# Values of three attention branches with tokens stationary, joined in two passes, and earlier last copies of a bank in the groups of seven products

## The chip, the cores and the metric

One core of one Trainium2 chip runs the whole program. The metric is device time in microseconds, from one launch, lower is better. TensorE (PE) does the matrix products, VectorE (DVE) and ScalarE (ACT) do the elementwise work, GpSimd (POOL) clears a few pads, SyncE (SP) issues the loads.

## The reference, cut to what matters

Two layers over 512 tokens with 1024 features, in float32. Each layer is half a SwiGLU step, a mixer of three attention branches, and another half SwiGLU step:

```
h = h + 0.5 * SwiGLU_1(RMSNorm(h))
u = RMSNorm(h);  z = u @ w_in        # a_q a_k a_v | b_q b_k b_v b_f | c_q c_k c_v | gates
A: differential attention (4 heads of 128), B: forgetting attention (8 heads of 64),
C: stick-breaking attention (8 heads of 64), all causal
m = sum_i sigmoid(gate_i) * (o_i @ proj_i);  h = h + m @ w_out
h = h + 0.5 * SwiGLU_2(RMSNorm(h))
```

Each of the queries, keys and values of a branch has 512 columns. The row scale of RMSNorm (`rstd`) is one number a token, and the gain is folded into `u`.

## The kernel before, in words

**Layout and precision.** Activations stand as features x tokens: 128 partitions, 512 token columns, eight such tiles for 1024 features. A float32 product is made of three rounded products (`three`, lines 713 to 717): each factor is kept as a rounded part (`_hi`) and the rest (`_lo`), and hi x hi, hi x lo and lo x hi are added in one PSUM bank. ACT makes the rounded part and DVE the rest, of weights too: `split(k)` is one ACT copy and one DVE subtraction of 128x1024 for one weight slot. There are three slots, each holding one *unit*, the 8 blocks of 128x128 that make 128 output columns of `w_in`. A unit on PE is 24 products of 512 columns.

**A tile of the mixer.** There are four tiles a layer, each with 128 columns of every branch (one head pair of B and of C, one head of A), and two layers, so eight tiles in all. Each tile has nine units: c_q, c_k, c_v, b_q, b_k, b_v, a_q, a_k, a_v (a letter for the branch). Their banks alternate between 0 and 1. When a unit is done, DVE's `take` multiplies the bank by `rstd` into one of two staging tiles. Queries and keys then get `qk_hi` on ACT (four copies of 64x512 for b and a) and `qk_lo` on DVE (two subtractions of 64x512), and `scores` waits on `qk_set` for both of its branch. Values stand as features x tokens after the unit but are needed as tokens x features: `turn_values` transposes the staging tile by four float32 transposes into the bank AUX, and `values_hi` and `values_lo` round it.

**Orders written by hand.** PE, ACT and DVE each have an order written out (`heads` and `rest_of_tile` in each engine's block), and each engine runs its order strictly. On PE the attention steps (`stick_scores` for C, `scores` for A and B, `turn_probs`, ten transposes of the weights; `weighted`, the product with the values) are placed between blocks of the units, so that ACT and DVE make the softmax or the stick-breaking weights while PE works on units. `weighted(branch, 1)` is followed on ACT by `output_rest(1)` and on DVE by `output_whole(1)`, which add the two halves of a result.

**Groups of seven products.** In the SwiGLU parts and for the gates, a 2x2 scheme needs seven products in place of eight (`pair`, line 760; `product` is 12 products of 256 columns). Products 0, 2, 4 and 6 add to one bank, and after 0, 2 and 4 ACT copies the bank away (`snap` 0, 2 and 3, line 1388; snap 1 is for another bank); PE waits for the copy before it adds the next one. ACT also makes the weight pieces of the next group (`piece_hi`), which wait for DVE's sums of weights. `pair_hi` (line 1394) is ACT's order for the SwiGLU, `gates_hi` for the gates.

Of the kernel before, what the change touches and what calls it, by code (L numbers as in the profile page):

```python
# [194 lines left out]
def trunk(nc, x, stream, params, const, const_r, const_b, out):  # L195
    ctx = ExitStack()
    with ctx:
# [12 lines left out]
        O_HI, O_LO = 0, 3 * NT * SEQ  # L210
        QK = 2 * O_LO
# [74 lines left out]
        def val_block(branch, part, j):  # L286
            return val(branch, part)[:, j * P:(j + 1) * P]
# [168 lines left out]
        mean_log, row_rstd = stat[:, 0:2], stat[:, 2:4]  # L456

# [58 lines left out]
        turned = sem("turned")  # L516
# [191 lines left out]
        def _(pe):  # L708
            c = Counts(pe, [acc_lo_set, g_part_set, snap_set, w_set, u_set, acc_set, rstd_set, hid_set, g_set, h_set, wf_set, staged,
                            rows_set, qk_set, v_set, max_set, prob_set, pt_set, o_sq, o_rstd, o_norm,  # L710
# [280 lines left out]
            def turn_values(st):  # L991

                for j in range(NQ):
                    last = pe.transpose(ps[:, AUX, j * P:(j + 1) * P], tile(st)[:, j * P:(j + 1) * P], ident)  # L994
                last.then_inc(turned, 1)
# [7 lines left out]
            def weighted_whole():  # L1003

                pe.wait_ge(v_set, c.next(v_set))

                pe.wait_ge(o_whole_set, c.next(o_whole_set))
                for j in range(NQ):
                    pe.wait_ge(pt_set, c.next(pt_set))
                    n, w_hi_j, w_lo_j = wide_keys(j)  # L1010
                    last = three(ps[:, OB, SEQ - n:SEQ], val_block(0, 0, j), val_block(0, 1, j), w_hi_j, w_lo_j,
                                 start=j == 0, stop=j == NQ - 1)
                last.then_inc(o_mm, 1)

            def weighted(branch, hd, before=True):

                if hd == 0:
                    pe.wait_ge(v_set, c.next(v_set))
# [7 lines left out]
                for j in range(NQ):  # L1026
                    pe.wait_ge(pt_set, c.next(pt_set))
                    n, w_hi_j, w_lo_j = wide_keys(j)
                    v = val_block(branch, hd, j)
# [20 lines left out]
            def unit(k, first_block=0, end=UNIT, first=False, before=True):  # L1050

                if first_block == 0 and (k > 1 or k == 0 and before):

                    pe.wait_ge(staged, c.next(staged, 1 if k else 2))
                last = u_unit(k % 2, k % SLOTS, (first_block, end), first)
# [3 lines left out]
            def rest_of_tile(unit):  # L1059

                unit(0)
                turn_probs(1)
                turn_values(0)
                unit(1, 0, 3)
                weighted(1, 1)
                scores(0, 0)
                unit(1, 3, 7)
                scores(0, 1)
                unit(1, 7)
                c.skip(max_set, NQ)  # L1070

            def heads(before):

                if before:
                    rest_of_tile(unit)
                    unit(2)
                    turn_probs(0)
                    unit(3, 0, 3)
                    weighted_whole()
                    unit(3, 3, 5)  # L1080
                else:
                    unit(0, first=True, before=False)
                    pe.wait_ge(const_set, 1)
                    sum_of_squares()
                    unit(1, 0, 3)
                    forget()
                    unit(1, 3)
                    unit(2)
                    pe.wait_ge(pads_set, c.next(pads_set, 4))
                stick_scores(0)  # L1090
                if before:
                    unit(3, 5, 6)
# [5 lines left out]
                turn_values(0)  # L1098
# [12 lines left out]
                unit(7, 4)  # L1111
                unit(8, 0, 2)
                turn_probs(0)
                turn_values(1)
                unit(8, 2)
                weighted(1, 0)
# [5 lines left out]
            def mixer():  # L1122
                heads(False)
                for _t in range(1, NT):
                    heads(True)

                def gate(k, first_block=0, end=UNIT):
                    if (k, first_block) == (0, 0):
                        pe.wait_ge(staged, c.next(staged, 2))
                    last = u_unit(k, k, (first_block, end))  # L1130
                    if end == UNIT:
                        last.then_inc(unit_done, 1)

                rest_of_tile(gate)
                pe.wait_ge(v_set, c.peek(v_set))
                gate(2, 0, 7)
                turn_probs(0)
                gate(2, 7)
# [4 lines left out]
                weighted_whole()  # L1143
# [5 lines left out]
            def branch_product(k0, b0, of, n, k):  # L1149
# [3 lines left out]
                if b == 0:  # L1153
                    pe.wait_ge(w_set, c.next(w_set))
                at = (branch * NT + k) * SEQ
                last = three(ps[:, of[n], :], slot(w_hi, s, b), slot(w_lo, s, b),
                             area[:, O_HI + at:O_HI + at + SEQ], area[:, O_LO + at:O_LO + at + SEQ],
# [117 lines left out]
        def half_tile(hd):  # L1275

            return ps[:, AUX, :].rearrange("p (j e) -> p j e", j=NQ)[:, :, hd * HEAD:(hd + 1) * HEAD]

        def half_val(branch, hd, part):

            at = HEAD * (hd ^ part)
            return val(branch, hd).rearrange("p (j e) -> p j e", j=NQ)[:, :, at:at + HEAD]

# [1871 lines left out]
```

## Time and profile before

| what | value |
|---|---|
| median of 3 runs | 2438.66 us (2438.55 to 2438.97) |
| the profiled execution's own time | 2438.91 us |
| its span | 2437.1 us |
| PE busy | 2425.9 us, 15514 products |
| DVE busy | 2130.1 us |
| ACT busy | 1493.9 us |
| granted PE clock, mean | 0.999 |
| chain that ended last, share on PE | 94% |

Products are pipelined: the duration of one (390 ns for 512 columns) is longer than the distance between the starts of two. What a product costs is the distance of starts, which the rows of a timeline show. A merged row shows the start of the first and the time to the end of the last.

### The profile page before, as it was taken

How to read it: one execution, taken by the hardware profiler on the slowest of the kernel's cores; microseconds unless marked ns; L12 is line 12 of the kernel's file. 1: busy time of each engine (PE TensorE's matmuls, PEld its weight loads, DVE VectorE, ACT ScalarE, POOL GpSimd, SP SyncE). 2: the span in 40 equal slices, each digit the busy share in tenths (PEclk: the TensorE clock that was granted, in tenths of full speed). 3: DMA queues.
4: the chain of work that ended last, by engine and by line, in shares of the span. 5: the costliest groups of instructions: out<-in, count | busy, mean ns of one | idle time of the engine just before them, and what ended most of it. 6: DMA issues, size and time to landing. Idle time of an engine off the chain costs nothing.

```text
span 2437.1 us, 48108 instructions
## 1 busy us (share of the span) xinstructions
PE 2425.9 (100%) x15514; PEld 2210.7 (91%) x15514; DVE 2130.1 (87%) x3960; ACT 1493.9 (61%) x2917; POOL 4.0 (0%) x14
## 2 busy tenths in 40 slices
PE   9999999999999999999999999999999999999999
PEld 7999888888899889998889998888888998899988
DVE  8999878998898779998699997789998986899985
ACT  7666357888754456664366664578886554566643
POOL 0000000000000000000000000000000000000000
PEclk9999999999999999999999999999999999999999
DMA  4333332212232323233333323322212333233332
GB/s 168 108 103 104 113 97 69 77 55 78 62 113 79 112 87 105 104 106 117 102 103 106 103 95 106 103 79 61 72 60 70 105 106 102 87 107 104 117 113 78
DMA packets 64676, 233.72 MB, mean 96 GB/s; under 512 B 7168, under 2 KB 7552, under 8 KB 64512
## 3 DMA queue, kind: packets, MB, share of 16 engines
q1 hardware_dynamic: 64368, 231.58, 29.3%
q8 instruction: 85, 1.39, 0.2%
q14 instruction: 79, 0.65, 0.1%
q10 hardware_dynamic: 144, 0.10, 0.0%
HBM read 229.55 MB, written 2.10 MB: 95 GB/s over the span
## 4 chain that ended last, share of the span: by engine, by line
PE 94%; DVE 3%; ACT 1%; issue 1%; DMA 0%; DVEq 0%; SPq 0%; ACTq 0%
PE ps L715 29%; PE ps L717 29%; PE ps L716 29%; PE ps L988 2%; PE ps L1031 1%; PE ps L978 1%; PE ps L979 1%; PE ps L1030 1%; DVE w_lo L1990 1%; ACT w_hi L1293 0%; PE ps L994 0%; PE ps L1042 0%; PE ps L1043 0%; DMA h<-x 0%; DVE u_lo L1990 0%
## 5 line engine op out<-in xcount | busy, mean ns | idle before, releaser
L1293 ACT ACTIVATE w_hi<-w_raw 128x512 fp32r<-128x512 f32 (+1 forms) x874 | 624.1, 721 | 470.6 <-PE ps L717 231.3
L1990 DVE TENSOR_TENSOR w_lo<-w_raw,w_hi 128x512 fp32r<-128x512 f32 (+1 forms) x874 | 699.2, 805 | 108.2 <-ACT w_hi L1293 91.8
L715 PE MATMUL ps<-u_hi,w_hi 128*128 128x256 f32 (+1 forms) x2432 | 786.1, 323 | 0.6 <-DVE w_lo L1990 0.6
L717 PE MATMUL ps<-u_hi,w_lo 128*128 128x256 f32 (+1 forms) x2432 | 781.0, 321 | 0.0
L716 PE MATMUL ps<-u_lo,w_hi 128*128 128x256 f32 (+1 forms) x2432 | 780.2, 321 | 0.0
L716 PE MATMUL ps<-area,w_hi 128*128 128x256 f32 (+1 forms) x1778 | 583.4, 328 | 0.0
L715 PEld LDWEIGHTS ps<-u_hi,w_hi 128*128 128x128 f32 x2432 | 463.3, 190 | 37.4 <-issue 2.3
L717 PEld LDWEIGHTS ps<-u_hi,w_lo 128*128 128x128 f32 x2432 | 463.2, 190 | 35.1
L716 PEld LDWEIGHTS ps<-u_lo,w_hi 128*128 128x128 f32 x2432 | 463.5, 191 | 32.8
L715 PE MATMUL ps<-area,w_hi 128*128 128x512 f32 (+1 forms) x1414 | 482.0, 341 | 2.4 <-ACT scratch_whole L1392 1.8
L717 PE MATMUL ps<-area,w_lo 128*128 128x512 f32 (+1 forms) x1414 | 480.1, 340 | 0.0
L716 PEld LDWEIGHTS ps<-area,w_hi 128*128 128x128 f32 x1778 | 338.1, 190 | 29.0
L715 PEld LDWEIGHTS ps<-area,w_hi 128*128 128x128 f32 x1414 | 268.2, 190 | 34.2 <-ACT scratch_whole L1392 1.8
L717 PEld LDWEIGHTS ps<-area,w_lo 128*128 128x128 f32 x1414 | 268.1, 190 | 29.6
L715 PE MATMUL ps<-v_area,w_hi 128*128 128x256 f32 x880 | 249.3, 283 | 0.0
L717 PE MATMUL ps<-v_area,w_lo 128*128 128x256 f32 x880 | 249.0, 283 | 0.0
L1392 ACT ACTIVATE scratch_whole<-ps 128x256 f32<-128x256 f32 x376 | 141.6, 377 | 159.9 <-PE ps L717 158.3
L715 PEld LDWEIGHTS ps<-v_area,w_hi 128*128 128x128 f32 x880 | 168.9, 192 | 0.2
L717 PEld LDWEIGHTS ps<-v_area,w_lo 128*128 128x128 f32 x880 | 168.9, 192 | 0.0
L1293 ACT ACTIVATE area<-scratch_whole 64x512 fp32r<-64x512 f32 (+1 forms) x202 | 123.7, 627 | 25.4 <-DVE scratch_whole L2896 11.8
L716 PE MATMUL ps<-v_area,w_hi 128*128 128x256 f32 x440 | 124.5, 283 | 0.0
L1990 DVE TENSOR_TENSOR area<-scratch_whole,area 64x512 fp32r<-64x512 f32 (+1 forms) x120 | 82.3, 685 | 16.1 <-ACT area L1293 14.0
(220 smaller groups left out, 2909.4 us busy)
## 6 DMA issues: line engine op xcount, KB each, us to landing
w_raw<-weights SPq DMA_DIRECT2D x432, 512.0 KB, 3.7
h<-x SPq DMA_DIRECT2D x4, 512.0 KB, 6.4
out<-scratch_whole SPq DMA_DIRECT2D x8, 256.0 KB, 2.0
scratch_whole<-const_b SPq DMA_DIRECT2D x1, 512.0 KB, 9.6
scratch_whole<-const_r SPq DMA_DIRECT2D x1, 192.0 KB, 8.9
cst<-const SPq DMA_DIRECT2D x1, 137.0 KB, 8.0
par<-params ACTq DMA_DIRECT2D x1, 98.0 KB, 4.5
```

Source lines behind the costliest of these rows:

```text
L715: pe.matmul(dst, hi, x_hi, start=start, stop=False, **kw)
L716: pe.matmul(dst, hi, x_lo, start=False, stop=False, **kw)
L717: return pe.matmul(dst, lo, x_hi, start=False, stop=stop, **kw)
L978: pe.matmul(dst, q_twice(branch, hd)[:, m], k_both(branch, hd)[:, 0:n], start=True, stop=False)
L979: pe.matmul(dst, q_rest(branch, hd)[:, m], k_bias(branch, hd)[:, 0:n], start=False, stop=True).then_inc(score_set, 1)
L988: last = pe.transpose(ps[:, SB0 + j, (i - j) * P:(i - j + 1) * P], prob[buf][:, at:at + P], ident)
L1030: pe.matmul(ps[:, OB, SEQ - n:SEQ], v, w_hi_j, start=j == 0, stop=False)
L1031: last = pe.matmul(ps[:, OB, SEQ - n:SEQ], v, w_lo_j, start=False, stop=j == NQ - 1)
L1293: return act.activation(dst, src, ACT.Copy)
L1392: act.activation(to, half_bank((of or banks(s))[2 if n == 1 else 0]), ACT.Copy).then_inc(snap_set, 1)
L1990: return dve.tensor_tensor(dst, src, hi_part.bitcast(F32), ALU.subtract)
```

## The change: what it does

It has two parts.

**One: values.** The three value units of a tile are joined. The stationary operand is now a block of 128 tokens of `u` (hi or lo), the moving one is the weights of all three branches, 384 columns, so the result comes out as tokens x features and `turn_values` is gone. With 8 feature blocks and 4 token blocks these are 32 steps of three products (`value_steps`), in two passes: token blocks 0 and 1, then 2 and 3. At feature block 2 the 384 weight columns wrap around the end of the slots, and the step is made of three products of 256 columns and three of 128. `values_hi` and `values_lo` now read four banks, in halves of 128x128 and 128x256, and scale by `token_rstd`, one number a partition, which PE gets once a layer by four transposes of `rstd` (`turn_rstd`). The stream of weights has a new order: c_q, c_k, the joined values in three units, b_q, b_k, a_q, a_k. Staging is by `take(k, bank, scale)`: queries in staging tile 0, keys in 1. All three hand-written orders of a tile change with it.

**Two: last copies.** In `pair_hi` for the first group of a SwiGLU, and in `gates_hi` for its first two groups, `snap` 3 comes ahead of the copy of weight piece 3 (and, in the very first group of the program, ahead of piece 2).

PE's order, the middle of a tile:

```
                     diff_norm()
-                unit(3, 6 if before else 0)
-                unit(4, 0, 6)
+                value_steps(20 if before else 11, 30, before)
+                turn_probs(0)
+                value_steps(30, 32, before)
                 ...
-                turn_values(0)
+                own = (AUX, 0, 1, AUX) if before else (0, AUX, 1, AUX)
+                unit(own[0], 2, 0, 5)
+                weighted(t, 2, 0, before)
+                stick_scores(1)
+                unit(own[0], 2, 5)
+                unit(own[1], 0)
                 turn_probs(0)
-                unit(4, 6)
-                unit(5, 0, 4)
-                weighted(2, 0, before)
-                stick_scores(1)
-                unit(5, 4)
-                unit(6, 0, 7)
+                unit(own[2], 1, 0, 5)
+                weighted(t, 2, 1)
+                scores(1, 0)
+                unit(own[2], 1, 5)
+                bank_read(1 if before else 2)
+                unit(own[3], 2, 0, 3)
                 turn_probs(0)
-                unit(6, 7)
-                unit(7, 0, 4)
-                weighted(2, 1)
-                scores(1, 0)
-                ...
```

ACT's order, after the stick-breaking of the second head:

```
                 act.preload_act_table_set(LN_EXP)
-                qk_hi(1, 2, 4)
+                qk_hi(1, 0, 0)
                 split(2)
                 turned_hi(0)
                 ...
                 turned_hi(3)
+                qk_hi(1, 2, 1)
                 split(0)
                 output_rest(1)
```

DVE's order at the same place:

```
                 output_whole(0)
-                qk_lo(1, 0, 3)
                 stick_runs(0)
                 ...
                 stick_weights(3)
-                take(5, 1.0)
+                banks = (AUX, 0, 1, AUX) if before else (0, AUX, 1, AUX)
+                take(0, banks[0], SCALE)
                 rows(t * 2, 1, 0)
-                qk_lo(1, 2, 4)
                 split(2)
+                qk_lo(1, 0, 0)
                 turned_lo(0)
                 ...
                 turned_lo(3)
-                take(6, SCALE)
+                take(1, banks[1], 1.0)
                 split(0)
                 output_whole(1)
+                qk_lo(1, 2, 1)
                 block_max(0, 0)
```

The new function on PE, and part two in `pair_hi`:

```
+            def value_steps(begin, end, before):
+                for n in range(begin, end):
+                    late, m = divmod(n, 2 * UNIT)
+                    k, j = m // 2, 2 * late + m % 2
+                    ...
+                    for first, after in ((0, 2), (2, 3)) if k == 2 else ((0, 3),):
+                        ...
+                        pe.matmul(dst, x_hi, w_hi[:, of], start=k == 0, stop=False, skip_group_check=True)
+                        pe.matmul(dst, x_lo, w_hi[:, of], start=False, stop=False, skip_group_check=True)
+                        last = pe.matmul(dst, x_hi, w_lo[:, of], start=False, stop=k == UNIT - 1, skip_group_check=True)

                 piece_hi(2, raws(s))
+                if first and not early:
+                    product_done()
+                    product_done()
+                    snap(s, 3)
                 hidden_hi(at - 2 * SEQ)
-                product_done()
+                if not first:
+                    product_done()
                 piece_hi(3, raws(s))
-                product_done()
-                snap(s, 3)
+                if not first:
+                    product_done()
+                    snap(s, 3)
```

## Rows read from the trace of the kernel before

**Rows 1.** The page: span, and busy time by engine.

```profile
span 2437.1 us, 48108 instructions
PE 2425.9 (100%) x15514; PEld 2210.7 (91%) x15514; DVE 2130.1 (87%) x3960; ACT 1493.9 (61%) x2917; POOL 4.0 (0%) x14
```

**Rows 2.** Waits of PE: total us, times, longest us.

```profile
PE ps L715 <- ACT scratch_whole L1392: 1.8, 2, 1.6
```

**Rows 3.** Timeline of PE, values turned: start us, us, engine, line, operation.

```profile
383.68 0.39 PE L717 MATMUL ps<-u_hi,w_lo 128*128 128x512 f32 x1
...
384.36 0.39 PE L717 MATMUL ps<-u_hi,w_lo 128*128 128x512 f32 x1
384.60 0.60 PE L994 MATMUL ps<-cst,scratch_whole 128*128 128x128 f32 x4
385.03 1.25 PE L988 MATMUL ps<-cst,scratch_whole 128*128 128x128 f32 x10
386.04 0.47 PE L715 MATMUL ps<-u_hi,w_hi 128*128 128x512 f32 x1
```

**Rows 4.** Timeline of PE, a later tile, the middle of it.

```profile
533.67 0.33 PE L1030 MATMUL ps<-area,v_area 128*128 128x384 f32 x1
533.84 0.34 PE L1031 MATMUL ps<-area,v_area 128*128 128x384 f32 x1
...
534.50 0.28 PE L1042 MATMUL ps<-area 128*128 128x256 f32 x1
...
543.29 1.25 PE L988 MATMUL ps<-cst,scratch_whole 128*128 128x128 f32 x10
...
549.10 0.28 PE L978 MATMUL ps<-area 128*128 128x256 f32 x1
```

**Rows 5.** Timeline of ACT in the same stretch.

```profile
540.40 2.31 ACT L1293 ACTIVATE area<-scratch_whole 64x512 fp32r<-64x512 f32 x4
542.74 1.06 ACT L1293 ACTIVATE w_hi<-w_raw 128x1024 fp32r<-128x1024 f32 x1
...
549.30 0.59 ACT L1656 ACTIVATE w_raw<-ps 64x512 f32<-64x512 f32 x1 [2.35 <-PE ps L1031]
```

**Rows 6.** Timeline of DVE in the same stretch.

```profile
538.37 1.00 DVE L2580 TENSOR_TENSOR_SCAN scratch_whole<-scratch_whole,masks 128x127 f32<-128x127 f32 x2
...
542.87 0.68 DVE L2510 SCALAR_TENSOR_TENSOR scratch_whole<-ps,rstd 128x512 f32<-128x512 f32 x1
...
544.11 1.39 DVE L1990 TENSOR_TENSOR area<-scratch_whole,area 64x512 fp32r<-64x512 f32 x2
545.52 1.23 DVE L1990 TENSOR_TENSOR w_lo<-w_raw,w_hi 128x1024 fp32r<-128x1024 f32 x1
546.66 1.68 DVE L1990 TENSOR_TENSOR area<-ps,area 128x512 fp32r<-128x512 f32 x4
548.26 0.68 DVE L2510 SCALAR_TENSOR_TENSOR scratch_whole<-ps,rstd 128x512 f32<-128x512 f32 x1
...
550.10 0.69 DVE L2625 TENSOR_TENSOR w_raw<-ps,w_raw 64x512 f32<-64x512 f32 x1
```

**Rows 7.** Timeline of PE at the start of the program.

```profile
3.18 5.58 PE L1225 MATMUL ps<-area 128*128 128x512 f32 x14 [3.18 <-issue]
8.60 0.40 PE L715 MATMUL ps<-u_hi,w_hi 128*128 128x512 f32 x1
```

**Rows 8.** Timeline of PE in the first group of seven products.

```profile
51.62 0.28 PE L717 MATMUL ps<-u_hi,w_lo 128*128 128x256 f32 x1
53.50 0.39 PE L715 MATMUL ps<-area,w_hi 128*128 128x256 f32 x1 [1.60 <-ACT scratch_whole L1392]
```

**Rows 9.** The same, first group of a later SwiGLU.

```profile
918.81 0.28 PE L716 MATMUL ps<-u_lo,w_hi 128*128 128x256 f32 x1
918.93 0.28 PE L717 MATMUL ps<-u_hi,w_lo 128*128 128x256 f32 x1
919.36 0.38 PE L715 MATMUL ps<-area,w_hi 128*128 128x256 f32 x1
```

More of the change, by code:

```diff
@@ L1048, in diff_norm, with unit @@
                 pe.matmul(ps[:, bank, :], ones_r[:], o_sq_lo, start=False, stop=True).then_inc(o_ms, 1)
[L1050 to L1055, printed above, removed]
+            def unit(bank, k, first_block=0, end=UNIT, first=False):
+                last = u_unit(bank, k, (first_block, end), first)
@@ L1117, in heads @@
+                unit(own[2], 1, 5)
+                bank_read(1 if before else 2)
+                unit(own[3], 2, 0, 3)
+                turn_probs(0)
+                unit(own[3], 2, 3)
+                weighted(t, 1, 0)
                 scores(1, 1)
@@ L1122, in mixer @@
             def mixer():
[L1123 to L1136, printed above, removed]
+                heads(0, False)
+                for t in range(1, NT):
+                    heads(t, True)
+                rest_of_tile(NT - 1, unit)
+                bank_read()
+                unit(2, 2, 0, 7)
                 turn_probs(0)
-                gate(2, 7)
+                unit(2, 2, 7)
                 pe.wait_ge(o_set, c.peek(o_set, 3 * NT - 2))
@@ L1602, in key_bias, with qk_hi @@
                         hi(k_bias(branch, hd)[half(1 - hd), :], key_sums[half(1 - hd), :])
-            def qk_hi(branch, which, k, takes=1):
-                act.wait_ge(staged, c.next(staged, takes))
+            def qk_hi(branch, which, k):
+                act.wait_ge(staged, c.next(staged))
                 for hd in range(2):
-                    src = tile(k % 2)[half(hd), :]
+                    src = tile(k)[half(hd), :]
                     if which == 0:
@@ L2463, in forget @@
                 dve.wait_ge(rstd_set, c.next(rstd_set))
-                stage_qk(2, 0, 0)
+                take(0, 0, SCALE, first=True)
+                split(0)
+                qk_lo(2, 0, 0)
                 y, soft, neg, run = tile(3), tile(2), tile(6), tile(4)
@@ L2475, in forget @@
                 dve.wait_ge(vec_done, c.next(vec_done))
-                take(1, 1.0)
+                take(1, 1, 1.0, first=True)
+                split(1)
                 dve.wait_ge(forget_out, layer * 2 + 1)
@@ L2499, in sums_of_forget, with take @@
                 dve.wait_ge(vec_done, c.next(vec_done))
-            def stage(k, scale):
-                take(k, scale)
-                split(k % SLOTS)
-            def take(k, scale):
-                if k >= 2:
+            def take(k, bank, scale, first=False):
+                if not first:
                     dve.wait_ge(qk_set, c.peek(qk_set, 0))
                 dve.wait_ge(unit_done, c.next(unit_done))
-                dve.scalar_tensor_tensor(tile(k % 2), ps[:, k % 2, :], scale, rstd[:], ALU.mult, ALU.mult
-                                         ).then_inc(staged, 1)
-            def stage_qk(branch, which, k):
-                stage(k, SCALE if which == 0 else 1.0)
-                qk_lo(branch, which, k)
+                dve.scalar_tensor_tensor(tile(k), ps[:, bank, :], scale, rstd[:], ALU.mult, ALU.mult).then_inc(staged, 1)
             def qk_lo(branch, which, k):
@@ L2613, in output_lo @@
             def output_lo(branch, t):
-                at = (t + branch * NT) * SEQ
+                rounded, rest = (area[:, o_at(branch, t, part):o_at(branch, t + 1, part)] for part in range(2))
                 src = o_whole[:]
@@ L2703, in heads @@
                 stick_weights(3)
-                take(5, 1.0)
+                banks = (AUX, 0, 1, AUX) if before else (0, AUX, 1, AUX)
+                take(0, banks[0], SCALE)
                 rows(t * 2, 1, 0)
-                qk_lo(1, 2, 4)
                 split(2)
+                qk_lo(1, 0, 0)
                 turned_lo(0)
@@ L3099, in weight_stream, with unit @@
         for t in range(NT):
-            for name in "cba":
-                for which in range(3):
-                    parts.append(columns(w_in, branch[name] + which * 512 + t * P))
+            def unit(name, which):
+                return columns(w_in, branch[name] + which * 512 + t * P)
+            values = np.concatenate([unit(name, 2) for name in "abc"], 0).transpose(1, 2, 0, 3)
+            parts += [unit("c", 0), unit("c", 1), values.reshape(P, 3, UNIT, P).transpose(1, 0, 2, 3)]
+            parts += [unit(name, which) for name in "ba" for which in range(2)]
         proj = np.concatenate([a[f"proj_{'abc'[b]}"][n].reshape(NT, P, ND, P) for b in TAIL_ORDER], 0)
```

254 lines of the change are left out of this document (142 added, 112 removed).

## The prediction

> **What bounds the kernel now.** I read the page's busy times first: PE has work in 2425.9 of 2437.1 us [rows 1]. A busy PE here means products that overlap, so I looked next at the waits of PE. Only 1.8 us in two places stand against ACT [rows 2], and in the timeline of the mixer one product starts as soon as the last lets it. Before is therefore PE's own list of products, one after the other. That gives two rules for the change. What it takes from PE's list is gained in full. And every wait that it puts into PE's order is lost in full, since there is no slack elsewhere on PE to give it back. The profiled execution took 2438.91 us, 1.8 us more than its span, and the median of the runs is 2438.66 us; I add to 2438.9.
>
> **PE's list, part one.** A product of 512 columns starts 0.227 us after the one before (384.36 - 383.68, three starts) [rows 3], one of 384 columns 0.17 (533.84 - 533.67; between the neighbours 0.227 and 0.120 I take 0.173) [rows 4], one of 256 columns 0.120 (918.93 - 918.81) [rows 9]. A float32 transpose of 128 columns takes 0.108 (385.03 - 384.60, four starts) [rows 3].
> - Removed in a tile: three value units, 3 x 24 x 0.227 = 16.34 us, and 12 transposes, 1.30 us.
> - Added in a tile: 28 steps x 3 x 0.173 = 14.53 us, 4 steps x 3 x 0.120 = 1.44 us, and 12 products with 128 moving columns of the rounded type, at a price that the trace does not show.
>
> The price of those twelve: the columns alone, by the slope between 256 and 512, would give 0.120 - 0.053 = 0.067. At the other end, they cost no less than a 512-column product, 0.227, if narrow products of this type are streamed slowly. Nearest is the float32 transpose of the same width, 0.108, and I take 0.11. The tile then changes by -17.64 + 15.97 + 1.32 = -0.35 us, eight tiles by -2.8 us; the ends are -6.9 and +8.5 us. The new transposes of `rstd` are four a layer, 0.9 us in all with `forget`'s surroundings unchanged. Sum of the list: -1.9 us. The banked gain from the transposes (10.4 us in eight tiles) is mostly eaten by more and shorter products, each of which carries a fixed 13 ns (0.120 less 256 columns at 0.107).
>
> The Trainium skill ("TensorE: Matmul & The Clock Gate", Back-to-back issue gap) gives a warm distance of N/2.4 + 2.5 ns, 56 ns for 128 columns. This trace disagrees where both can be compared: 120 ns for 256 columns and not 109. By the page the twelve narrow products would be 5.2 us cheaper over the eight tiles.
>
> **The wait that the new orders make.** `scores(1, 0)` on PE waits on `qk_set` for the queries and keys of branch B, that is for DVE's `qk_lo(1, 2, 1)`. In DVE's new order this stands behind `output_whole(1)`, which needs ACT's `output_rest(1)`, which needs PE's `weighted(t, 2, 1)`. And `weighted(t, 2, 1)` is what stands directly ahead of `scores(1, 0)` on PE. So PE must stop there in every tile, whatever the speeds: at least for ACT's copy, DVE's sum and DVE's two subtractions. From the rows that is 1.0 us to the start of the sum (550.10 - 549.10), 0.7 and 1.4 us [rows 4 to 6]: 3.1 us a tile is the low end.
>
> The true length comes from the whole chain, counted from s, the start of `stick_scores(1)`. Before, s is 534.50 and `scores(1, 0)` starts at 549.10, 14.6 us later [rows 4], with 16 blocks of units, one set of transposes and one `weighted` in between. The new order has 3 + 8 + 5 = 16 blocks and the same others there, so PE again arrives at s + 14.6. The others, with distances of starts where operations follow each other:
> - s + 1.0: DVE's `output_whole(0)` (as 550.10 - 549.10), over at s + 1.7 [rows 4, 6].
> - Stick-breaking on DVE, 538.37 to 542.87, 4.5 us, over at s + 6.2. Before, `qk_lo(1, 0, 3)` stood ahead of it; that is gone from here.
> - `take(0)` of b_q, 0.6 us: s + 6.8 [rows 6]. Only now can ACT begin `qk_hi(1, 0, 0)`. Before, ACT copied b_k here, from a staging tile filled long before (540.40, 2.3 us before `take(5)`).
> - ACT: four copies 2.34 us, s + 9.2; `split(2)` 1.0 us, s + 10.2 [rows 5].
> - DVE: rest of `split(2)` 1.15, `qk_lo(1, 0, 0)` 1.4, four `turned_lo` 1.6, `take(1)` of b_k 0.65: s + 15.0 [rows 6]. All of these stand in the way of b_k, whose unit PE ended at about s + 8.8.
> - ACT: `qk_hi(1, 2, 1)` 2.34, `split(0)` 1.05: s + 18.4.
> - DVE: `split(0)` 1.2, `output_whole(1)` 0.7, `qk_lo(1, 2, 1)` 1.4: s + 21.8.
>
> PE waits 21.8 - 14.6 = 7.2 us a tile, of which some 0.3 us falls ahead of `weighted(t, 2, 1)` (its first `turned_lo` is done at s + 13.5). Eight tiles: 57.6 us. Before, the same `qk_lo` was over at 545.5, 3.6 us ahead of its use [rows 4, 6]. Behind the stopped `scores(1, 0)` are queued all later blocks of the tile; nothing else on PE can run.
>
> **Smaller waits.** DVE loses one `take` a branch (0.6 us each) but gains eight smaller operations on the values. They stand ahead of `weighted(t, 2, 0)`, and the wait there on `v_set` covers all four token blocks; counting from `stick_scores(0)` I find DVE 0.3 to 0.4 us late in six tiles. For the last head of B, `qk_hi(0, 0, 0)` starts about 1 us later behind the transposed weights than before, while PE comes 1.1 us sooner: some 0.4 us in eight tiles. In the first tile of a layer `split(1)` stands ahead of `qk_hi(2, 2, 1)`: 0.3 us, twice. Together 6 us; the bounds are 0, if the slack is a little larger, and 20 us, at 2.5 us a tile. The loads don't enter: as many, of the same size, over three slots, and the slots are needed later than before.
>
> **Part two.** In the first group PE stood from 51.62 to 53.50, 1.76 us over the 0.120 us that is due, and the next product started 0.1 us late as well [rows 8]. `snap` 3 came at 53.09 behind three copies of 0.5 us; without them it comes 1.6 us sooner, product 4 having long ended: -1.5 us. In the later groups the same wait is small, 0.43 us in place of 0.12 at 918.93, and 0.1 us at the restart [rows 9]; there are seven like it, three at the first groups of the other SwiGLUs and four in the gates, of 0.28 to 0.42 us, and one copy of 0.5 us less hides them all: -2.4 us. The weight pieces moved back by 0.4 us are for products at least one product (1.4 us) away, so nothing takes their place. Sum -3.9 us, bounds -1.5 and -5.
>
> **Sum without the clock.** 2438.9 - 1.9 + 57.6 + 6 - 3.9 = 2496.7 us.
>
> **The clock.** With one stop of 7 us in every tile the granted clock comes into play. At the start PE had done nothing, and its first 14 products of 512 columns took 5.42 us (8.60 - 3.18) and not the 3.18 that the warm distance gives: the lower level, 1.2 GHz, for most of them, and 2.25 us lost [rows 7]. The longest idle time since, 1.60 us, did not bring the clock down (0.999 over the span) [rows 8]. A stop of 7 us is four times that, and I take it that the clock falls in each and costs what it cost at the start: 8 x 2.25 = 18 us. Bounds: 0 and 30 us.
>
> The Trainium skill (the same page, Part 1: The HAM clock gate) says that the throttled state is the default and activity is what lifts it, so that an idle PE falls back; by it the 18 us are due. No row of this trace shows a fall after idleness.
>
> Forecast: 2496.7 + 18 = 2515 us, 3.1% slower.
>
> **The rivals.**
> - *The clock stays up.* Everything as above without the last term: 2497 us. For it: 1.60 us did no harm. Against it: the cold start. Chance 0.28.
> - *The short wait.* ACT or DVE reaches the keys sooner than I count, and PE waits only for the unavoidable 3.1 us: 2438.9 - 1.9 + 24.8 + 2 - 3.9 = 2460 us. For it: DVE and ACT have idle time elsewhere. Against: the chain is of data and strict orders, and each link has a row. Chance 0.06.
> - *More waits than counted.* The narrow products cost 0.227 (+11 us), or the smaller waits reach their 20 us: 2530 to 2540 us. Chance 0.12.
> - *Not slower.* The place is again `scores(1, 0)`. If the chain from s took less than 14.6 us, PE would never stand there, and the list and part two would be all: 2438.9 - 1.9 - 3.9 = 2433 us. It decides at a chain 7.2 us shorter than mine. The order `weighted`, `output_whole`, `qk_lo`, `scores` excludes it unless I misread an order. Chance 0.04.
>
> The forecast itself has 0.5. About 0.2% (4.9 us) is what a measurement of this kernel can tell from no change. Faster 0.03, within it 0.01, slower 0.96. The range runs from 2486 (clock up, a chain 1.4 us shorter a tile) to 2533 (forecast with the smaller waits at their upper end): 8 in 10.
>
> **What would show it.** In the waits of PE a new largest entry: the first product of `scores` (the line of 978) on DVE's L1990, or its successor, 16 times at most and about 7 us each in eight. In the timeline, products behind it at 0.427 us distance for some microseconds, or at 0.227 if the clock stays. The value steps at 0.173, the twelve narrow products at their true price. PE idle in the first group down from 1.6 to some 0.2 us. I am wrong if PE shows no entry of microseconds on `scores`, and wrong in the clock if the stops are there and the products behind them are at 0.227.

## The result

The changed kernel takes 2525.96 us (median of 5 runs, 2525.22 to 2527.8), the kernel before 2438.64 us (5 runs, 2438.48 to 2438.97): a ratio of 1.036 with a 95% interval of 1.0348 to 1.0371, 87.3 us slower. The prediction was 2515 us, with 2486 to 2533 as its range.

The page of the changed kernel, against [rows 1]: PE has 200 more instructions and is busy 26 us longer, and it now stands idle for 74 us.

```profile
span 2526.0 us, 48501 instructions
PE 2452.1 (97%) x15714; PEld 2244.8 (89%) x15714; DVE 2127.6 (84%) x3960; ACT 1503.3 (60%) x2943; POOL 4.0 (0%) x14
```

The waits of PE (total us, times, longest us), against [rows 2]. L994 is the first product of `scores`, L1071 that of `weighted`, L731 the first line of `three`, and L2036 is DVE's subtraction `lo`:

```profile
PE ps L994 <- DVE area L2036: 54.8, 8, 6.9
PE ps L1071 <- DVE area L2036: 5.0, 8, 0.6
...
PE ps L1071 <- DVE area L2644: 2.8, 8, 0.7
PE ps L731 <- ACT scratch_whole L1421: 0.9, 1, 0.9
```

One row holds most of the loss: eight stops, one in every tile, at the place that the forecast named. The timeline of PE around the second of them (start us, us, engine, line, operation, idle before and its releaser) shows what it does:

```profile
477.65 0.28 PE L1083 MATMUL ps<-area 128*128 128x256 f32 x1
...
491.26 0.50 PE L1071 MATMUL ps<-area 128*128 128x512 f32 x1
...
492.53 0.28 PE L1072 MATMUL ps<-area 128*128 128x256 f32 x1
499.67 0.58 PE L994 MATMUL ps<-area 128*128 128x256 f32 x1 [6.85 <-DVE area L2036]
...
501.33 0.63 PE L994 MATMUL ps<-area 128*128 128x512 f32 x1
501.75 0.63 PE L995 MATMUL ps<-area 128*128 128x512 f32 x1
```

`stick_scores(1)` starts at 477.65, which is the s of the forecast's chain. The last product of `weighted(t, 2, 1)` starts at 492.53 and `scores(1, 0)` at 499.67, 7.14 us later where 0.12 is due. Behind the stop the products of 512 columns follow each other at 0.42 us (501.75 - 501.33) and not at 0.227.

DVE in the same stretch, against [rows 6]:

```profile
478.47 0.68 DVE L2665 TENSOR_TENSOR w_raw<-ps,w_raw 64x512 f32<-64x512 f32 x1 [1.31 <-ACT w_raw L1703]
...
483.58 0.67 DVE L2554 SCALAR_TENSOR_TENSOR scratch_whole<-ps,rstd 128x512 f32<-128x512 f32 x1
...
487.96 1.23 DVE L2036 TENSOR_TENSOR w_lo<-w_raw,w_hi 128x1024 fp32r<-128x1024 f32 x1 [3.19 <-ACT w_hi L1322]
...
492.11 0.68 DVE L2554 SCALAR_TENSOR_TENSOR scratch_whole<-ps,rstd 128x512 f32<-128x512 f32 x1
496.24 1.23 DVE L2036 TENSOR_TENSOR w_lo<-w_raw,w_hi 128x1024 fp32r<-128x1024 f32 x1 [3.45 <-ACT w_hi L1322]
497.50 0.69 DVE L2665 TENSOR_TENSOR w_raw<-ps,w_raw 64x512 f32<-64x512 f32 x1
498.22 1.39 DVE L2036 TENSOR_TENSOR area<-scratch_whole,area 64x512 fp32r<-64x512 f32 x2
```

And ACT, against [rows 5]:

```profile
484.29 2.56 ACT L1322 ACTIVATE area<-scratch_whole 64x512 fp32r<-64x512 f32 x4 [1.77 <-DVE scratch_whole L2554]
486.87 1.06 ACT L1322 ACTIVATE w_hi<-w_raw 128x1024 fp32r<-128x1024 f32 x1
...
492.83 2.31 ACT L1322 ACTIVATE area<-scratch_whole 64x512 fp32r<-64x512 f32 x4 [3.59 <-DVE scratch_whole L2554]
495.15 1.06 ACT L1322 ACTIVATE w_hi<-w_raw 128x1024 fp32r<-128x1024 f32 x1
```

The subtraction that releases PE is the row at 498.22, the last link of a chain in which the engines take turns: DVE waits 3.19 us for ACT, then ACT 3.59 us for DVE's `take(1)` at 492.11, then DVE 3.45 us for ACT, and PE 6.85 us for DVE. The waiting goes round the engines, 17 us in all within 22, and no engine's busy share shows it.

The clock, in windows (us, then busy time of PE, PEld, DVE, ACT and POOL, then PEclk, the granted clock as a share of full speed, DMA share and GB/s):

```profile
492.90:499.80 6.90, 0.14 (x1) 0.14 (x1) 3.29 (x4) 4.49 (x7) 0.00 (x0) 0.83 0.10 36
499.90:501.50 1.60, 1.60 (x7) 1.60 (x8) 0.73 (x4) 0.60 (x3) 0.00 (x0) 0.50 0.35 143
501.50:504.00 2.50, 2.50 (x8) 1.92 (x7) 2.07 (x9) 2.02 (x6) 0.00 (x0) 0.50 0.00 0
```

The clock falls to 0.50 (1.2 GHz) during the stop and stays there for 4.6 us of work behind this stop, and for 3.6 to 5.8 us over the eight.

Where the 88.9 us between the two spans (2526.0 - 2437.1) went, from the distances of starts:

| part | us |
|---|---|
| eight stops at `scores(1, 0)`, 7.13 us less 0.12 each | 56.1 |
| lower clock behind them: 32 products behind each restart take 65.74 us, at full clock 8 x 6.16 = 49.3 | 16.5 |
| PE's list in the mixers: value steps and `rstd` 70.98 us a layer in place of 288 x 0.2275 + 4.58 = 70.1, so 1.8 more; 26 in place of 40 slow 512-column products behind transposes, 1.2 less | 0.6 |
| waits of `weighted`: the 16 gaps ahead of it take 10.01 us a layer, 3.64 are due | 12.7 |
| `turn_probs`, 400 transposes in 45.0 us, before 42.0 | 3.0 |
| outside the mixers (part two), 1815.9 us before, 1814.1 after | -1.9 |
| not assigned | 1.9 |

The slow products of the third row: a product of 512 columns that comes directly behind transposes starts its successor 0.31 us later and not 0.23. The stretch outside the mixers is counted between the starts of the same products: up to the first 512-column product of a mixer, and on from the first 256-column product of its last weighted product (350.51 and 660.73 us in the first layer before).

### The profile page after: what moved, and what is told of

It reads as the page before. It is cut to its first block, busy times and chain, and to the rows that moved or that the text cites. A ratio compares the mean times of both kernels' runs of the same rounds, so it can differ in the third digit from the quotient of the medians.

```text
span 2526.0 us, 48501 instructions
## 1 busy us (share of the span) xinstructions
PE 2452.1 (97%) x15714; PEld 2244.8 (89%) x15714; DVE 2127.6 (84%) x3960; ACT 1503.3 (60%) x2943; POOL 4.0 (0%) x14
## 4 chain that ended last, share of the span: by engine, by line
PE 84%; DVE 7%; issue 4%; ACT 3%; DVEq 0%; DMA 0%; SPq 0%; ACTq 0%
PE ps L731 25%; PE ps L732 25%; PE ps L733 25%; DVE area L2036 2%; PE ps L1032 2%; PE ps L1033 2%; PE ps L1034 2%; ACT area L1322 1%; ACT w_hi L1322 1%; PE ps L1004 1%; DVE w_lo L2036 1%; PE ps L994 1%; PE ps L995 1%; PE ps L1071 1%; DVE scratch_whole L2619 1%
## 5 line engine op out<-in xcount | busy, mean ns | idle before, releaser
L2036 DVE TENSOR_TENSOR w_lo<-w_raw,w_hi 128x512 fp32r<-128x512 f32 (+1 forms) x874 | 699.4, 806 | 170.5 <-ACT w_hi L1322 153.7
L731 PE MATMUL ps<-u_hi,w_hi 128*128 128x256 f32 (+1 forms) x2240 | 712.2, 318 | 0.0
L732 PE MATMUL ps<-u_lo,w_hi 128*128 128x256 f32 (+1 forms) x2240 | 708.5, 316 | 0.0
L733 PE MATMUL ps<-u_hi,w_lo 128*128 128x256 f32 (+1 forms) x2240 | 708.2, 316 | 0.0
L731 PE MATMUL ps<-area,w_hi 128*128 128x512 f32 (+1 forms) x1414 | 482.1, 341 | 1.0 <-ACT scratch_whole L1421 0.9
L731 PEld LDWEIGHTS ps<-u_hi,w_hi 128*128 128x128 f32 x2240 | 429.9, 192 | 27.6 <-DVE w_lo L2036 0.5
L733 PEld LDWEIGHTS ps<-u_hi,w_lo 128*128 128x128 f32 x2240 | 429.0, 192 | 28.1
L732 PEld LDWEIGHTS ps<-u_lo,w_hi 128*128 128x128 f32 x2240 | 429.5, 192 | 27.0
L731 PEld LDWEIGHTS ps<-area,w_hi 128*128 128x128 f32 x1414 | 268.1, 190 | 32.5 <-DVE w_lo L2036 1.6
L731 PE MATMUL ps<-v_area,w_hi 128*128 128x256 f32 x880 | 249.3, 283 | 0.0
L731 PEld LDWEIGHTS ps<-v_area,w_hi 128*128 128x128 f32 x880 | 168.9, 192 | 0.4 <-DVE w_lo L2036 0.2
L994 PE MATMUL ps<-area 128*128 128x256 f32 (+2 forms) x128 | 46.2, 378 | 54.8 <-DVE area L2036 54.8
```

The source lines that it names most:

```text
L731: pe.matmul(dst, hi, x_hi, start=start, stop=False, **kw)
L732: pe.matmul(dst, hi, x_lo, start=False, stop=False, **kw)
L733: return pe.matmul(dst, lo, x_hi, start=False, stop=stop, **kw)
L994: pe.matmul(dst, q_twice(branch, hd)[:, m], k_both(branch, hd)[:, 0:n], start=True, stop=False)
L2036: return dve.tensor_tensor(dst, src, hi_part.bitcast(F32), ALU.subtract)
```

## The experiments

In each the kernel before was timed beside the others; its median was between 2438.6 and 2439.3 us.

**Is the stop the chain, and one order of DVE its cause?** Three kernels differ from the changed one in DVE's order only. The first takes the keys' subtraction ahead of the weight piece and of the sum of the outputs:

```diff
                 take(1, banks[1], 1.0)
+                qk_lo(1, 2, 1)
                 split(0)
                 output_whole(1)
-                qk_lo(1, 2, 1)
```

> The changed kernel with one line of DVE's order moved: qk_lo(1, 2, 1) stands directly behind take(1), ahead of split(0) and output_whole(1). ACT's and PE's orders are as changed. My theory: the chain to the keys of B loses DVE's wait for ACT's copy of split(0) and output_rest(1), its own 1.2 and 0.7 us, so PE's stop at scores(1, 0) goes from 7.0 to about 4.0 us in eight tiles: 2526 - 24 = 2502 us with the clock still falling in each, 2484 us if a stop of 4 us is too short for it. Rival: the stop is set by ACT alone (its copies of the keys stand behind the transposed weights), and DVE's order does nothing: 2526 us.

Measured: 2501.54 us (2500.1 to 2501.84; ratio 1.0256, 1.0239 to 1.0273), span 2499.6. All eight stops are now 4.07 us, of which PE is idle for 3.79. That is the case with the falling clock: behind every one of these stops there were products at 0.427 us. The windows behind the second stop:

```profile
493.30:494.60 1.30, 0.89 (x6) 0.90 (x7) 1.27 (x2) 0.60 (x2) 0.00 (x0) 1.00 0.00 0
494.60:497.50 2.90, 2.90 (x9) 2.29 (x8) 2.81 (x11) 1.83 (x6) 0.00 (x0) 0.52 0.39 143
```

The clock was still full when PE restarted at 493.7 and fell 1.0 us later.

The second moves `take(1)` as well, ahead of the transposed weights:

```diff
+                take(1, banks[1], 1.0)
                 turned_lo(0)
                 ...
                 turned_lo(3)
-                take(1, banks[1], 1.0)
+                qk_lo(1, 2, 1)
                 split(0)
                 output_whole(1)
-                qk_lo(1, 2, 1)
```

> The changed kernel with DVE's order mended further: take(1) of b_k ahead of the four turned_lo, and qk_lo(1, 2, 1) directly behind them, ahead of split(0). The other engines' orders are as changed. My theory: counted from stick_scores(1) the keys of B are ready at about 17.4 us in place of 22.1, weighted(t, 2, 1) comes 0.65 us later, and PE stops some 2 us at scores(1, 0), too short for the clock to fall: 2526 - 8 x 4.9 + 8 x 0.65 - 17.6 = 2474 us. That would still be 35 us slower than before, so a wait remains. Rival: the loss is in the products of the joined values, which this doesn't touch, and the waits move elsewhere: above 2500 us.

Measured: 2477.5 us (2476.61 to 2481.29; ratio 1.0162, 1.0145 to 1.0179), span 2476.3, clock 0.998. The stops are 1.88 to 1.89 us from start to start, of which PE is idle for 1.6. The clock fell behind two of the eight, in the third tile of the first layer and the fourth of the second. The stops of the second tile and of the third, and the clock behind each:

```profile
488.04 0.39 PE L994 MATMUL ps<-area 128*128 128x256 f32 x1 [1.60 <-DVE area L2036]
563.86 0.58 PE L994 MATMUL ps<-area 128*128 128x256 f32 x1 [1.61 <-DVE area L2036]
...
488.00:491.00 3.00, 2.96 (x15) 2.62 (x16) 2.93 (x7) 1.26 (x5) 0.00 (x0) 1.00 0.28 37
563.90:566.90 3.00, 3.00 (x10) 2.71 (x11) 2.94 (x9) 1.26 (x5) 0.00 (x0) 0.50 0.17 51
```

The gap ahead of `weighted(t, 2, 1)` grew from 0.52 to 1.2 us, since its first transposed weights stand behind the take.

The third puts the take where DVE has nothing to do (the 3.19 us ahead of 487.96 above); PE ends that unit within this time, at about s + 9.0:

```diff
                 rows(t * 2, 1, 0)
+                take(1, banks[1], 1.0)
                 split(2)
                 qk_lo(1, 0, 0)
                 turned_lo(0)
                 ...
                 turned_lo(3)
-                take(1, banks[1], 1.0)
+                qk_lo(1, 2, 1)
                 split(0)
                 output_whole(1)
-                qk_lo(1, 2, 1)
```

> Only DVE's order differs from the changed kernel: the take of branch B's key unit stands ahead of the weight piece of slot 2 (DVE has nothing to do for 3.2 us there while PE has already ended that unit), and the subtraction on the keys ahead of slot 0 and of the sum of the outputs. The chain then reaches the scores 1.1 us sooner than in the run where the take stood only ahead of the transposed weights, and the four transposed weights aren't pushed back by 0.7 us. Theory (the stop is that chain and nothing else): the stop shrinks from 1.89 to 0.6 to 0.8 us, the wait ahead of weighted(2,1) from 0.97 to 0.3, the clock stays up: 2477.5 - 8 x 1.15 - 8 x 0.7 - 2.9 = about 2460 us. Rival: DVE or ACT are late for another reason (their own load in the whole tile): then what is won here comes back as a longer wait at the next weighted products, and the time stays at 2470 or above.

Measured: 2463.76 us (2463.64 to 2464.24; ratio 1.0102, 1.0086 to 1.0119), span 2462.0, clock 1.000. Two lines of one engine's order, moved up, with the same operations on every engine, bring back 62.2 of the 87.3 us. DVE's rows of the second tile:

```profile
478.41 0.69 DVE L2554 SCALAR_TENSOR_TENSOR scratch_whole<-ps,rstd 128x512 f32<-128x512 f32 x1 [1.88 <-PE ps L733]
...
480.86 1.38 DVE L2036 TENSOR_TENSOR area<-scratch_whole,area 64x512 fp32r<-64x512 f32 x2
482.27 1.68 DVE L2036 TENSOR_TENSOR area<-ps,area 128x512 fp32r<-128x512 f32 x4
483.98 1.39 DVE L2036 TENSOR_TENSOR area<-scratch_whole,area 64x512 fp32r<-64x512 f32 x2
```

The keys are ready at 485.4 and not behind the sum of the outputs, and PE stands there for 0.86 us only:

```profile
485.43 0.39 PE L994 MATMUL ps<-area 128*128 128x256 f32 x1 [0.86 <-DVE area L2036]
```

The stop fell from 7.13 to 1.13 us, 8 x 6.0 = 48 us, and the clock's 16.5 us went with it: 64.5, against 64.0 between the spans. It came out 4 us above the expected 2460, as the stop was 1.1 and not 0.7 us.

**Is it PE's idleness that brings the clock down?** Products into a free bank fill the stop; they add work and change no order of ACT or DVE:

```diff
                 weighted(t, 2, 1)
+                bank_read(1 if before else 2)
+                for _ in range(22):
+                    pe.matmul(ps[:, own[3], :], u_hi[:, 0:P], u_hi[:, 0:SEQ], start=True, stop=True)
                 scores(1, 0)
                 unit(own[2], 1, 5)
-                bank_read(1 if before else 2)
```

> The changed kernel with 22 more products of 512 columns in each of the eight tiles, put where PE stops: behind weighted(t, 2, 1) and ahead of scores(1, 0). They write the bank that b_q has been taken from (the wait for that is moved ahead of them) and nothing reads them; the unit that follows there starts that bank anew. 22 x 0.227 = 5.0 us of work lies inside a stop of 7.0 us. My theory, that the stop is set by DVE's chain and that idleness in it brings the clock to its lower level: the stop ends when it did, some 2 us of idleness are left, no product behind it is at 0.427 us distance, and the time falls by the 17.6 us that the eight cold stretches lost: 2526 - 17.6 = 2508 us. Rival one, the clock falls for another reason (what ACT and DVE do there, or the load of the joined products): still 0.427, 2526 us. Rival two, PE's list is what bounds the tile and the stop is only where the profile puts its time: the 22 products are added in full, 2526 + 40 = 2566 us.

Measured: 2521.25 us (2521.07 to 2521.28; ratio 1.0338, 1.0321 to 1.0356), span 2519.3. A miss by 13 us, and an instructive one. With the 22 products PE is still idle for 1.55 us in the first tile of a layer and for 1.84 to 1.87 us in the other three (1.94 and 2.24 us from the start of the last added product to the scores). In the six places with some 1.85 us the clock still fell, 0.7 to 0.9 us behind the restart; in the two with 1.55 us it didn't. The second tile:

```profile
495.10:497.10 2.00, 0.25 (x2) 0.00 (x0) 1.96 (x3) 0.63 (x1) 0.00 (x0) 1.00 0.45 86
497.10:498.10 1.00, 0.91 (x6) 0.91 (x7) 0.40 (x4) 0.04 (x1) 0.00 (x0) 0.96 0.83 332
498.10:501.00 2.90, 2.90 (x9) 2.31 (x8) 2.47 (x12) 2.46 (x8) 0.00 (x0) 0.50 0.02 7
```

So this run alone could not say whether idleness or the place is the cause. The same kernel with 31 products, which leave nothing empty, could:

> The changed kernel with 31 products of 512 columns, into a bank that is free, between the last weighted product of the second head of branch C and the stopped scores; in the run with 22 such products PE still stood idle for 2.24 us of the 7.13, and the clock fell in six of eight places. 31 x 0.227 = 7.04 us fill the stop to within 0.1 us. If idleness is what brings the clock down, all 17.6 us come back and nothing else changes: 2526.0 - 17.6 = 2508.4 us, mean clock 0.998 or more, no product behind the restart at 0.427. Rival: the stretches at the lower level belong to the place in the program (the kind of work ahead of them or the restart after a wait), not to PE's idleness: then the time stays at 2519 to 2526 and the 0.427 rows remain.

Measured: 2512.08 us (2511.8 to 2512.26; ratio 1.0301, 1.0283 to 1.0318), span 2510.3, mean clock 1.000, and no product behind a restart at 0.427. The same stretch of the second tile:

```profile
497.50:501.00 3.50, 3.50 (x19) 3.04 (x19) 2.91 (x14) 2.29 (x8) 0.00 (x0) 1.00 0.21 87
```

Idleness is the cause: place, order and what ACT and DVE do are those of the changed kernel, and only the idle time is gone. 13.9 us came back by the medians, 15.7 by the spans, with 0.9 us more spent in the eight places (7.16 to 7.50 us from the last weighted product to the scores). The 17.6 us in the expectations were a little too many; the 32 products give 16.5, and the run 14.8 to 16.6.

**Are the remaining waits latencies that other work can cover?** On top of the kernel with the take first, PE's order only:

```diff
-                unit(1, 1, 0, 3)
+                unit(1, 1, 0, 4)
                 weighted(t, 1, 1)
                 scores(0, 0)
-                unit(1, 1, 3, 7)
+                unit(1, 1, 4, 7)
...
-                unit(own[2], 1, 0, 5)
+                unit(own[2], 1, 0, 7)
                 weighted(t, 2, 1)
                 scores(1, 0)
-                unit(own[2], 1, 5)
+                unit(own[2], 1, 7)
```

> The run with the take put first (2463.8 us), and two groups of products in PE's order moved ahead of waiting ones: two more blocks (6 products, 1.36 us) ahead of the last weighted product of the second head of branch C, and one more (0.68 us) ahead of that of branch B. In the trace of the run without them PE still stands 1.0 us at the first scores of B, 0.29 us at the weighted product before it and 0.79 us at the one of B, in every tile. Theory (these are latencies that work placed ahead covers): 8 x (1.0 + 0.29 + 0.68) = 15.8 us less, 2448 us; what then remains over the kernel before is the list and the transposes that wait. Rival: DVE is too late in the tile as a whole, and each wait that is covered comes back at the next place (the transposed probabilities, the next weighted product): 2456 us or more.

Measured: 2460.31 us (2460.28 to 2460.41; ratio 1.0086, 1.0069 to 1.0103): 3.5 us less, not 15.8. The rival holds. The covered places did shrink, by 7.7 us at `scores` and 7.9 us at `weighted` over both layers, but the transposes of the probabilities went from 45.1 to 53.8 us, and 3.0 us came at a product of the units behind the value steps. The ten transposes behind `scores(1, 0)` take 2.23 us where they took 1.25 [rows 4], since they start before their last inputs are made (DVE scales the last of the probabilities until 490.38):

```profile
488.86 2.23 PE L1004 MATMUL ps<-cst,scratch_whole 128*128 128x128 f32 x10
```

Between `scores(1, 0)` and these transposes there were six blocks of units and are now four, and the softmax on DVE and ACT takes as long as before. A tile has a fixed number of blocks, and what is placed ahead of one wait is missing ahead of the next.

**Part two alone.** The changed kernel with part two undone:

> The changed kernel with part two undone: pair_hi and gates_hi as before. Forecast of the text: part two is worth 3.9 us, so 2530 us. What the two traces say by the time of the same marks: the stretch outside the mixers is only 2.4 us shorter after the change, and the first SwiGLU not at all, so 2528.4 us. Rival: part two does nothing or harm, 2526 us or less.

Measured: 2527.07 us (2525.86 to 2528.47; ratio 1.0364, 1.0347 to 1.0381), 1.1 us above the changed kernel, which is no more than these two kernels spread. The lower clock is part of that spread: in this run's trace the eight stops are the same 7.13 us, but the 32 products behind each take 62.2 us in all, 12.9 over full clock, where the changed kernel's trace has 16.5. What the clock doesn't touch can be compared: outside the mixers the same products take 1815.7 us here and 1814.1 with part two, 1.6 us. (The 2.4 us of the expectations, against the kernel before, come to 1.9 between the starts of the same products.) Then part two on the kernel before, in three forms, 11 runs each, the order of `gates_hi` as in the change in all of them:

```diff
     def pair_hi(s, at, first=False, early=False):
         ...
         piece_hi(1, raws(s))
+        if early:               # the program's first group
+            product_done(); product_done(); snap(s, 3)
         piece_hi(2, raws(s))
+        if first and not early: # first groups of the other SwiGLUs
+            product_done(); product_done(); snap(s, 3)
```

> The kernel before with part two of the change alone (the last copy of a bank ahead of a weight piece in the first group of each SwiGLU and in the gates). From the two traces part two is worth 2.4 us: 0.5 at each later place, nothing in the first SwiGLU, where 1.8 us at its first stop are given back at two others: 2438.65 - 2.4 = 2436.2 us. Rival (as predicted from the kernel before, each place paying in full): 2434.8 us. Second rival: the gain seen beside part one depends on part one's timing: 2438 or above.

Measured: 2437.69 us (2437.08 to 2438.23) against 2439.29 (2438.57 to 2440.34, 27 runs); ratio 0.9992, 0.9983 to 1.0001.

> Part two on the kernel before, but in the very first group the last copy stands behind the third weight piece as in all later groups, not ahead of it. One copy of a piece (0.4 to 0.5 us) returns to the stop at 51.6 us; if the stop at 62.4 us shrinks by as much, since ACT's pieces come as soon as before, the time is that of the whole part two, 2436.2. If it doesn't shrink: 2436.6.

Measured: 2437.77 us (2437.34 to 2438.63), ratio 0.9994, 0.9985 to 1.0003.

> Part two on the kernel before without its edit of the program's very first group. The stop of 1.76 us at 51.6 comes back. If the stop of 1.09 us at 62.4 and the one of 0.2 us at 56.4 were its price, they go, and the time is within 0.5 us of the whole part two: 2436.2 to 2436.7. Rival (the stop at 62.4 has nothing to do with the first group's order): 1.5 us slower than the whole part two, 2437.7.

Measured: 2437.82 us (2437.43 to 2438.88), ratio 0.9994, 0.9985 to 1.0003.

All three are 1.5 to 1.6 us below the kernel before, at the edge of what can be told from no change, and within 0.13 us of each other. So the edit of the very first group is worth nothing. The traces say the same: from PE's 151st product to its 501st, a stretch that takes in both groups, the kernel before takes 45.23 us, the whole part two 45.21, the form without the copy ahead of the third piece 45.20 and the form without the first group's edit 45.23. The timeline of PE says why: with the edit undone, the stop of [rows 8] is back and the one ten microseconds later is gone; with it, PE stands there instead. First the whole part two, then the form without the first group's edit:

```profile
62.91 0.28 PE L717 MATMUL ps<-u_hi,w_lo 128*128 128x256 f32 x1
64.12 0.38 PE L715 MATMUL ps<-area,w_hi 128*128 128x256 f32 x1 [0.93 <-ACT scratch_whole L1392]
```

```profile
51.56 0.28 PE L717 MATMUL ps<-u_hi,w_lo 128*128 128x256 f32 x1
53.45 0.39 PE L715 MATMUL ps<-area,w_hi 128*128 128x256 f32 x1 [1.60 <-ACT scratch_whole L1392]
...
63.49 0.28 PE L717 MATMUL ps<-u_hi,w_lo 128*128 128x256 f32 x1
63.62 0.28 PE L715 MATMUL ps<-area,w_hi 128*128 128x256 f32 x1
```

No version was found that beats the kernel before by more than the measurement is uncertain; part two alone is the best that was run.

## Why the prediction was right

The step that it rests on, the chain to `scores(1, 0)`, came out link by link. Counted from s = 477.65: the sum of the outputs starts at 0.8 (forecast 1.0), `take(0)` ends at 6.6 (6.8), ACT's copies of the queries end at 9.2 (9.2), `split(2)` at 10.3 (10.2), `take(1)` at 15.1 (15.0), ACT's `split(0)` at 18.6 (18.4), the keys' subtraction at 22.0 (21.8). PE had ended its work ahead of the scores at s + 15.0 (14.6). The stops came to 56.1 us. The forecast's 57.6 had in it some 0.3 us a tile ahead of `weighted(t, 2, 1)`, which the table books under `weighted`; with these 2.3 us the found value is 58.4. That it is this chain, and not DVE's or ACT's load, the three orders show: the same instructions, with the take at s + 9.0 (478.41, s being 469.42 in that trace) in place of s + 14.5, cost 48 us of stops less.

*The clock.* Forecast 18 us from the cold start of [rows 7], found 16.5 in this trace, and 12.9 behind equal stops in that of part two undone. The mechanism was right, and with the 31 products it is shown. The argument behind it was weaker than it looked: it said that 1.60 us of idleness did no harm and 7 us are four times that. One harmless case of 1.60 us was no proof that 1.60 us are harmless: by the idle time ahead of the scores, the clock fell behind none of two stops of 1.55 us, two of eight of 1.60 us, and all of those of 1.85 us (six), 3.79 us (eight) and 6.85 us (eight). The page "TensorE: Matmul & The Clock Gate" of the Trainium skill (Part 1: The HAM clock gate) has an idle PE fall back to the throttled state; this trace agrees, with PEclk at 0.50 behind each of the eight stops.

*PE's list*, forecast -1.9 us, found +0.6. The narrow product was estimated well, at 0.11, for a mean of 0.094. The narrow products of one step, and the 256-column products behind them:

```profile
451.62 0.22 PE L1032 MATMUL ps<-w_hi,u_hi 128*128 128x128 f32 x1
451.68 0.28 PE L1033 MATMUL ps<-w_hi,u_lo 128*128 128x128 f32 x1
451.79 0.27 PE L1034 MATMUL ps<-w_lo,u_hi 128*128 128x128 f32 x1
451.90 0.33 PE L1032 MATMUL ps<-w_hi,u_hi 128*128 128x256 f32 x1
452.07 0.28 PE L1033 MATMUL ps<-w_hi,u_lo 128*128 128x256 f32 x1
```

The three products start 0.06, 0.11 and 0.11 us ahead of the next, but the product of 256 columns behind them then takes 0.17 and not 0.12. The sum missed such restarts, which come behind the narrow products and behind transposes: the value steps take 70.6 us a layer and not the 4 x (84 x 0.173 + 12 x 0.12 + 12 x 0.11) = 69.2. The removed transposes were priced well at 5.2 us a layer: 4.6 by their own distances of starts, and 0.6 for the slow products behind them that went too. By its list alone the change gains nothing.

*The smaller waits* are the term that was mis-sized: forecast 6 us, found 13.4 without those ahead of `weighted(t, 2, 1)`: 10.4 at the other `weighted` and 3.0 at the transposes of the probabilities, which the forecast had at nothing. That is inside the stated 0 to 20. The forecast gave the last head of branch B "some 0.4 us in eight tiles"; that place alone costs 0.79 us in every tile, 6.3 us. PE and then DVE there, in the second tile:

```profile
440.73 0.39 PE L733 MATMUL ps<-u_hi,w_lo 128*128 128x512 f32 x1
441.74 0.50 PE L1071 MATMUL ps<-area 128*128 128x512 f32 x1 [0.63 <-DVE area L2036]
```

```profile
438.25 1.22 DVE L2036 TENSOR_TENSOR w_lo<-w_raw,w_hi 128x1024 fp32r<-128x1024 f32 x1
439.50 1.00 DVE L2569 TENSOR_SCALAR area<-w_lo_whole,cst 64x512 fp32r<-64x512 f32 x2
440.42 0.68 DVE L2665 TENSOR_TENSOR w_raw<-ps,w_raw 64x512 f32<-64x512 f32 x1
441.02 1.67 DVE L2036 TENSOR_TENSOR area<-ps,area 128x512 fp32r<-128x512 f32 x4
```

DVE works here without a gap and is late: `turned_lo` at 441.02 starts 10.4 us behind `scores(1, 1)`, in the kernel before 9.6 us. By the orders the reason is that both `qk_lo` of branch A now stand behind block maxima that one of them stood ahead of; that was not tried by itself. The late transposes are just ahead, one set in every tile (1.45 us where 1.01 to 1.09 are due). The other places are the first weighted product of a layer (0.91 us, twice), that of branch C in the other tiles (0.35 to 0.45 us) and its second head (0.29 us in each tile, which the forecast had named).

*Part two*, forecast -3.9 us, found -1.6 between the traces of the changed kernel with and without it, and -1.6 by the medians when alone. The step that failed is the one for the program's first group, -1.5 us, "so nothing takes their place". Something did: PE waits 0.93 us for ACT's copy at 64.12, a stop that is there only with the edit. That the pushed-back pieces delay the next group's copy is argued from ACT's order, not shown. The seven later places were counted for 2.4 us and gave some 1.2. The four of the gates gave 0.15 to 0.3 each. In the three SwiGLUs the first group came 0.4 us sooner, and each of the next two groups, 10 and 20 us later, lost 0.15 of it: something took their place here too.

The profiled execution took 2527.8 us, 13.1 above the sum of 2514.7: +2.5 in the list, +7.4 in the small waits, +2.0 in part two, +0.8 in the stops, -1.5 in the clock, and the 1.9 not assigned. All but the clock have one sign, so it isn't that errors cancelled. In the list it was the price of an operation in the steady row of its neighbours, without what it costs to come and go; in part two a stop that was removed and came back a group later. The range's upper end, 2533, isn't what its text says: the sum with the smaller waits at 20 us is 2529, still above the result.

## What to carry to other kernels

Where an engine runs an order written out by hand, a new order is to be read for the last producer ahead of each consumer, across engines, before its instructions are counted: here two lines on DVE decided 62 us, while PE's list, which the change was about, moved by less than 1. A wait covered by work taken from ahead of another wait isn't gone; the blocks of a tile against the sum of its latencies tell whether there is anything to win by moving them. And a stop of PE is to be counted with the lower clock behind it, about 2 us each here: in every case with 1.85 us of idleness and more, and in two of eight at 1.6.

## What the runs showed of the hardware

The granted clock need not fall in the stop itself. Behind the idle times of 1.85 us, and behind five of the eight of 3.79 us, it was still at full speed when PE restarted, and fell to 0.50 up to 1.0 us later, with PE fully at work (the windows at 494.60 and 498.10 above). A short stop can thus cost nearly as much as a long one: 32 products behind the restart, 6.16 us at full clock, took 7.7 to 7.8 us behind 1.85 us of idleness, 7.6 to 8.95 us behind 3.79 us, and 7.4 to 8.8 us behind 6.85 us.

Equal stops of 1.60 us didn't have equal results. The clock fell behind two of eight, in tiles that differ between the two layers, though the order of work is the same in both. Nor do equal executions agree: this kernel's took 2476.61 us at a mean clock of 0.999 and 2481.29 us at 0.997. So neither the length of such a stop nor its place in the program says whether it is followed by the lower clock; what does stays open.
